# The delta-rule scan: the second half-chunk's tokens kept in the other head's rows, half-chunks issued in turn, and state change and outputs interleaved over the array's quarters

## The reference

```python
def step(S, inp):
    r_t, w_t, k_t, v_t, kk_t, b_t = inp
    sa = jnp.einsum('bhvk,bhk->bhv', S, kk_t)
    S = S * w_t[:, :, None, :] - sa[..., None] * b_t[:, :, None, :] + v_t[..., None] * k_t[:, :, None, :]
    return S, jnp.einsum('bhvk,bhk->bhv', S, r_t)
```

## Time and profile before

| | us |
|---|---|
| median of 3 runs (lowest, highest) | 4899.13 (4895.42, 4918.35) |
| span of the profiled execution | 4902.0 |
| scan of layer 0, from the trace | 354 to about 1080 |
| scan of layer 1, from the trace | 2181 to about 2915 |
| PE busy, whole span | 4470.8 (91%) |
| DVE, ACT, POOL busy, whole span | 3140.0, 2151.1, 1188.4 |

### The profile page before, as it was taken

The page is one execution under the profiler, slowest core; times in us unless marked ns, Lnnn a source line. Parts: engine busy times, 40 slices in busy tenths (PEclk is TensorE's granted clock), DMA queues, the critical chain, the costliest instruction groups (busy, mean ns, idle before and its releaser), DMA issues. The chain is left out here.

```text
span 4902.0 us, 126091 instructions
## 1 busy us (share of the span) xinstructions
PE 4470.8 (91%) x55528; PEld 3812.3 (78%) x55528; DVE 3140.0 (64%) x4910; ACT 2151.1 (44%) x3962; POOL 1188.4 (24%) x863
## 2 busy tenths in 40 slices
PE   6989999989799969989989989799979988999999
PEld 6888888887588858878888878688857657888887
DVE  5436666669788874346666678889864476661752
ACT  2333443432288853334334342688843252331431
POOL 1002222222244420012223221444321000222221
PEclk9999999999899989999999999899989889999999
DMA  5421111123367664321111032567651003333332
GB/s 148 144 63 25 38 23 34 26 85 81 130 257 270 251 204 127 109 59 25 35 34 25 21 108 82 223 247 263 255 180 31 13 1 125 95 101 119 114 113 91
DMA packets 378284, 535.78 MB, mean 109 GB/s; under 512 B 117445, under 2 KB 301829, under 8 KB 349693
## 3 DMA queue, kind: packets, MB, share of 16 engines
q1 hardware_dynamic: 335645, 488.54, 30.8%
q0 software_dynamic: 40752, 33.95, 2.3%
q10 hardware_dynamic: 1344, 5.24, 0.3%
HBM read 569.43 MB, written 121.40 MB: 141 GB/s over the span
## 5 line engine op out<-in xcount | busy, mean ns | idle before, releaser
L289 PE MATMUL ps<-w_hi,xbT 128*128 128x512 f32 x1520 | 498.3, 399 | 19.8 <-DVE w L2835 19.8
L289 PE MATMUL ps<-hT,w_in 128*128 128x416 f32 (+1 forms) x2736 | 495.4, 340 | 4.1 <-DVE hT L3122 4.1
L289 PEld LDWEIGHTS ps<-hT,w_in 128*128 128x128 f32 x2736 | 458.9, 195 | 30.3 <-issue 19.2
L2835 DVE TENSOR_TENSOR w<-w,w_hi 128x2048 fp32r<-128x2048 f32 x190 | 425.6, 2280 | 2.2 <-ACT w_hi L2792 2.2
L1655 POOL TENSOR_TENSOR lm<-Ab,consts 116x416 f32<-116x416 f32 x240 | 255.8, 1073 | 435.9 <-PE ps L289 252.5
L289 PEld LDWEIGHTS ps<-w_hi,xbT 128*128 128x128 f32 x1520 | 288.4, 190 | 87.1 <-DVE w L2835 28.8
L2792 ACT ACTIVATE w_hi<-w 128x2048 fp32r<-128x2048 f32 x190 | 355.4, 1937 | 0.0
L289 PE MATMUL ps<-w,xbT 128*128 128x512 f32 x760 | 299.1, 394 | 0.0
L2866 DVE TENSOR_TENSOR w<-w,w_hi 128x2048 fp32r<-128x2048 f32 x95 | 221.7, 2333 | 95.3 <-ACT w_hi L2828 95.3
L289 PE MATMUL ps<-w_hi,actT 128*128 128x512 f32 x760 | 251.1, 391 | 5.0 <-DVE actT L2861 5.0
L289 PE MATMUL ps<-x1T,w_gate 128*128 128x512 f32 x1056 | 249.5, 393 | 3.2 <-DVE x L4052 1.6
(11 more groups left out here) (463 smaller groups left out, 10868.8 us busy)
## 6 DMA issues: line engine op xcount, KB each, us to landing
w<-in_moe_w_dram SPq DMA_DIRECT2D x192, 1024.0 KB, 12.5
w_gate<-in_w_gate_dram SPq DMA_DIRECT2D x44, 512.0 KB, 3.9
w_up<-in_w_up_dram SPq DMA_DIRECT2D x44, 512.0 KB, 3.9
w_down<-in_w_down_dram SPq DMA_DIRECT2D x44, 512.0 KB, 3.6
w_in<-in_w_in_dram SPq DMA_DIRECT2D x36, 512.0 KB, 4.5
w_out<-in_w_out_dram SPq DMA_DIRECT2D x24, 512.0 KB, 6.8
t_h<-x SPq DMA_DIRECT2D x20, 416.0 KB
kn<-t_kn SPq DMA_DIRECT2D x8, 1040.0 KB, 6.5
```

The costliest lines, as they stand in the source:

```text
L289: made = e.matmul(out, a, b, start=start, stop=stop)
L2835: e.tensor_tensor(w.lo, w.x, w.hf, ALU.subtract).then_inc(*P.c("moe_dve").tick(li, "w13", b, k))
```

## The change

In chunk 1 the tokens of head `o` now lie in the row half of the other head (`token_rows`), so chunk 0 uses the straight pair where chunk 1 uses the crossed one. Phases 11 to 13 issue the chunks in turn (`crossings`), so that four matmuls in a row are on four quarters; ACT takes both turned tensors after both are done. The turn of `hb0` leaves phase 14 and goes behind the level matmuls of phase 22 (`TURN0`), its ACT copy behind that level's `XX`, and phase 23 waits for it. Phases 28 and 31 interleave the state's change (bank `2d`) with the outputs (bank `2d+1`) in `step_rows`. Chunk 1's part of the right side from the values (`value_rows`) and its output from the old state (`state_output`) are made earlier and put away by ACT; DVE then adds the rest (`rh`, `ys`: two more DVE instructions in a step). The waits of `scan_free` become waits for whole groups.

```diff
-BY_ACT = {2, 3, 8, 9} | {13 + 3 * lv for lv in range(4)} | {25 + 4 * x + n for x in range(2) for n in (0, 1, 3)}
+TURN0 = 22
+STATE, INNER = slice(128, 384), slice(384, 512)
...
+def token_rows(o, ch):
+    return half_rows(o ^ ch)
+def crossings():
+    return [(j, ch, o) for j in range(4) for ch in range(2) for o in range(2)]
+def token_turns(P, d, at, x, step, view):
+    return [(P.ps[2 * d + ch][token_rows(o, ch), at + 64 * j:at + 64 * j + 64], view(x, slice(64 * o, 64 * o + 64), j, ch))
+            for j, ch, o in crossings()]
+def state_rows(P, d, m, S, ch):
+    return [(P.ps[2 * d + j % 2][half_rows(o ^ ch ^ j % 2), 64 * (j // 2):64 * (j // 2) + 64],
+             m.kr[64 * o:64 * o + 64, j, 0, H * ch:H * ch + H], S[64 * o:64 * o + 64, j, :], True, ch == 1)
+            for j in range(4) for o in range(2)]
+def value_rows(P, d, m, ch):
+    return [(P.ps[2 * d + j % 2][c, 64 * (j // 2):64 * (j // 2) + 64], m.ak[t, place(1, ch, j), 0, :],
+             m.vt[t, ch, 64 * j:64 * j + 64], ch == 1, True) for j, _, t, c in quarters(range(4))]
+def state_output(P, d, m, S, ch, j):
+    out = P.ps[2 * d + 1][:, STATE]
+    return [(out[half_rows(1 - o), 64 * j:64 * j + 64], m.kr[64 * o:64 * o + 64, j, 1, H * ch:H * ch + H],
+             S[64 * o:64 * o + 64, j, :], True, ch == 1) for o in range(2)]
+def step_rows(P, d, m, S, ch):
+    state, out, mats = P.ps[2 * d][:, STATE], P.ps[2 * d + 1][:, STATE], []
     for j in range(4):
         jc, u = slice(64 * j, 64 * j + 64), place(1, ch, j)
+        if ch == 0:
+            mats += state_output(P, d, m, S, ch, j)
+        for mat, w in ((0, m.ak), (1, m.ab)):
+            for o in range(2):
+                t = token_rows(o, ch)
+                x = m.vt[t, ch, jc] if mat == 0 else m.uu[t, split_columns(j)]
+                mats.append((state[64 * o:64 * o + 64, jc], m.tm[t, mat, ch, jc], x, mat == 0, mat == 1))
+            for o in range(2):
+                t = token_rows(o, ch)
+                x = m.vt[t, ch, jc] if mat == 0 else m.uu[t, split_columns(j)]
+                mats.append((out[half_rows(1 - o), jc], w[t, u, 1, :], x, ch == 1 and mat == 0, mat == 1))
     return mats
...
+        turns(e, P, token_turns(P, d, 0, rw.v, step, lambda x, q, j, ch: x[q, j, half(d, step, ch)]))
+        e.wait_ge(*dv.at(*key, "hb1"))
+        turns(e, P, token_turns(P, d, 256, m.hb, step, lambda x, q, j, ch: x[q, 1, j, H * ch:H * ch + H])
+              ).then_inc(*pe.tick(*key, 3))
+    if ph in (12, 13):
+        mat, use = 13 - ph, 2 * ph - 20
+        if ph == 12:
+            e.wait_ge(*dv.at(*key, "kr1"))
+            e.wait_ge(*ac.at(*key, "ev", 3))
+        else:
+            e.wait_ge(*dv.at(*key, "hb0"))
+            e.wait_ge(*dv.at(*key, "ev", 5))
+        mats = []
+        for j, ch, o in crossings():
+            q, at = slice(64 * o, 64 * o + 64), 2 * H * (place(1, ch, j) // 4 * 2 + j // 2)
+            mats.append((P.ps[2 * d + ch][token_rows(o, ch), at:at + 2 * H].rearrange("p (a t) -> p a t", a=2),
+                         m.hb[q, mat, j, H * ch:H * ch + H], m.kr[q, j, :, H * ch:H * ch + H], True, True))
+        mms(e, mats).then_inc(*pe.tick(*key, use))
...
-            mms(e, mats).then_inc(*pe.tick(*key, base))
+            made = mms(e, mats)
+            if ph == TURN0:
+                made = turns(e, P, token_turns(P, d, 4 * H, m.hb, step, lambda x, q, j, ch: x[q, 0, j, H * ch:H * ch + H]))
...
+            if ph == TURN0 + 1:
+                e.wait_ge(*ac.at(*key, "ev", 8))
             for n in range(4 if lv < 5 else 0):
...
+            if lv == 5 and m.chunks[0] == 1:
+                e.wait_ge(*ac.at(*key, "ev", 2))
+                e.wait_ge(*dv.at(*key, "ev", 7))
+                mats += value_rows(P, d, m, 1)
...
-                e.wait_ge(*ac.at(*key, "ev", use - 1))
+                e.wait_ge(*(ac if ch else dv).at(*key, "y", 0))
+            if ch == 1:
+                e.wait_ge(*ac.at(*key, "values"))
             e.wait_ge(*(dv.at(*key, "fS", x) if step or x else dv.at(li, d, "S0")))
-            mms(e, state_rows(P, d, m, S, ch, m.vt[:, ch, :])).then_inc(*pe.tick(*key, use))
+            mats = state_rows(P, d, m, S, ch)
+            if ch == 0:
+                rest = value_rows(P, d, m, ch)
+                mats = mats[0:4] + rest[0:4] + mats[4:8] + rest[4:8]
+            mms(e, mats).then_inc(*pe.tick(*key, use))
         if part == 1:
-            e.wait_ge(*ac.at(*key, "ev", use))
-            mms(e, [(P.ps[2 * d + j % 2][r, 64 * (j // 2):64 * (j // 2) + 64], m.TT[c, 4 * ch + j, :],
-                     m.rh[c, split_columns(j)], True, True) for j, o, r, c in quarters(range(4))]
-                ).then_inc(*pe.tick(*key, use + 1))
+            e.wait_ge(*(dv if ch else ac).at(*key, "rh", x))
+            mats = [(P.ps[2 * d + j % 2][t, INNER][:, 64 * (j // 2):64 * (j // 2) + 64], m.TT[c, 4 * ch + j, :],
+                     m.rh[c, split_columns(j)], True, True) for j, _, t, c in quarters(range(4))]
+            if ch == 1:
+                for j in range(4):
+                    mats += state_output(P, d, m, S, ch, j)
+            elif x == 0:
+                mats += value_rows(P, d, m, 1)
+            mms(e, mats).then_inc(*pe.tick(*key, use + 1))
         if part == 2:
-            b = scan_bank(P, d, step, use + 2)
-            mats = []
-            for j in range(4):
-                jc = slice(64 * j, 64 * j + 64)
-                mats += [(b[q, jc], m.tm[r, 0, ch, jc], m.vt[r, ch, jc], True, False) for q, r in ODD]
-                mats += [(b[q, jc], m.tm[r, 1, ch, jc], m.uu[r, split_columns(j)], False, True) for q, r in ODD]
-            e.wait_ge(*ac.at(*key, "ev", use + 1))
-            mms(e, mats).then_inc(*pe.tick(*key, use + 2))
-            mms(e, outputs(scan_bank(P, d, step, use + 3), m, S, ch, m.vt[:, ch, :])).then_inc(*pe.tick(*key, use + 3))
+            e.wait_ge(*ac.at(*key, "uu", x))
+            if ch == 1:
+                e.wait_ge(*ac.at(*key, "ys"))
+            elif x == 0:
+                e.wait_ge(*ac.at(*key, "values"))
+            mms(e, step_rows(P, d, m, S, ch)).then_inc(*pe.tick(*key, use + 2))
...
-        take(m.vt[0:HP].rearrange("p c n -> p (c n)"), scan_bank(P, d, step, 2)[0:HP, :], 2)
+        take(m.vt[0:HP], both[:, :, 0:256], 2, 3)
+        take(m.tm[0:HP, 1], both[:, :, 256:512], 3)
...
+    if ph == TURN0:
+        e.wait_ge(*dv.at(*key, "ev", 8 + 3 * level_of(TURN0)[0]))
+        take(m.tm[0:HP, 0], both[:, :, 4 * H:4 * H + 256], 8, 8 + 3 * level_of(TURN0)[0])
+    if ph == 25 and m.chunks[0] == 1:
+        e.wait_ge(*dv.at(*key, "T", 5))
+        e.activation(halves(m.rh)[0:HP], both[:, :, 0:128], ACT.Copy).then_inc(*ac.tick(*key, "values"))
...
+            if x == 0 and ch == 0:
+                e.activation(halves(m.rh)[0:HP], both[:, :, 0:128], ACT.Copy).then_inc(*ac.tick(*key, "values"))
...
+    if ph >= 26:
+        x, part = divmod(ph - 26, 3)
+        ch, use = m.chunks[x], 25 + 4 * x
+        if part == 0 and ch == 1:
+            e.wait_ge(*ac.at(*key, "values"))
+            e.wait_ge(*pe.at(*key, use))
+            e.tensor_tensor(halves(m.rh)[0:HP], halves(m.rh)[0:HP], P.banks[0:HP, 2 * d:2 * d + 2, 0:128], ALU.add).then_inc(
+                *dv.tick(*key, "rh", x))
+        if part == 2:
+            e.wait_ge(*pe.at(*key, use + 2))
+            e.tensor_tensor(m.S[1 - x], m.S[x], P.ps[2 * d][:, STATE].rearrange("p (j n) -> p j n", j=4), ALU.add).then_inc(
+                *dv.tick(*key, "S", x))
+            if ch == 1:
+                e.wait_ge(*ac.at(*key, "ys"))
+                e.tensor_tensor(m.ys[0:HP, 1, :], m.ys[0:HP, 1, :], P.ps[2 * d + 1][0:HP, STATE], ALU.add).then_inc(
+                    *dv.tick(*key, "y", x))
+            if x == 0:
+                e.wait_ge(*ac.at(*key, "f"))
+                e.wait_ge(*dv.at(*key, "S", 0))
+                shrink(1)
```

More of the change, by code:

```diff
@@ L1251, in scan_bank @@
     return P.ps[2 * d + use % 2]
[L1254 to L1259, removed]
 def squares(ps):
@@ L1318, in quarters @@
     return [(j, o, half_rows(o), half_rows(o ^ j % 2)) for j in js for o in range(2)]
[L1321 to L1331, removed]
@@ L1358, in scan_pe @@
         out = [scan_bank(P, d, step, use)[:, 0:416].rearrange("p (j t) -> p j t", t=C) for use in range(2)]
-        for use in range(2):
-            scan_free(e, P, li, d, step, use)
+        if step:
+            e.wait_ge(*dv.at(li, d, step - 1, "S", 1))
+            e.wait_ge(*(dv if m.chunks[1] else ac).at(li, d, step - 1, "y", 1))
         for j in range(4):
@@ L1367, in scan_pe @@
         e.wait_ge(*dv.at(*key, "kr0"))
[L1368 to L1387, removed]
-                     m.hb[q, mat, j, hs], m.kr[q, j, :, hs], True, True) for j in range(4) for q, r in ODD]
-                ).then_inc(*pe.tick(*key, use))
+        turns(e, P, token_turns(P, d, 0, rw.v, step, lambda x, q, j, ch: x[q, j, half(d, step, ch)]))
@@ L1405, in scan_pe @@
             if lv == 1:
```

(37 more changed lines are left out.)

48 lines of the change are left out of this document (15 added, 33 removed).

## The result

The changed kernel takes 4919.14 us (median of 20 runs, 4907.56 to 4942.78) against 4901.97 of the kernel before (20 runs, 4890.33 to 4921.78); the ratio is 1.0035, 95% interval 1.0025 to 1.0046. So it is 0.35% slower, clear of noise though inside the half per cent that the prediction calls no change, and 122 us above the forecast. The profiled execution of the changed kernel is the slowest of its twenty (4942.78 us, a span of 4941.0); the one of before lies near its median. Its granted clock over the whole program is 0.932, where the median of the twenty is 0.936 and the kernel before has 0.958. So the loss of clock that follows is in every execution, but the trace shows it some 20 us larger than the median execution has it ((0.936 - 0.932) x 4941).

What follows compares the result with a forecast made beforehand. PE was taken to bound the scan except where DVE sets the time up to the second `Ab`. Savings of 4.71 us a step, net 2.54, gave 102 us in 40 steps: span 4902.0 to 4800, time 4797 us, range 4735 to 4862.

Steps and rivals of the forecast that it cites:

- net sum of 2.54 us a step: Whole scan step: PE time saved less what waits take back, 2.54 us, or 102 us in 40 steps.
- the clock falls: Rival: long PE waits before the second `Ab` halve the clock; 4831 to 4874 us in part (0.10), slower each step (0.03).
- saving of 4.71: PE time saved per step by four quarters in phases 11 to 14, 28 and 31: 4.71 us, 188 in 40 steps.
- (1): Turns and first products ahead of the second `Ab`: DVE sets the time there, so 0 of 1.67 us counted.
- (2): Phase 13 waits for both `Ab`, not the first: 0.3 us a step lost (0 to 0.5).
- (3): Turn of `hb0` in phase 22, its copy delaying phase 23: covered by the `sig` to `kr0` chain, 0.45 us given back.
- (4): First chunk's end: state change complete only with the last matmul, DVE instructions follow; 0.3 us lost (0 to 1.3).
- (5): Before phase 28, PE waits for ACT's second copy behind `uu`: 0.35 us lost (0 to 0.4).
- (6): Two added DVE instructions, 0.42 us each, lie where DVE waits for PE: 0 lost (to 0.5).
- signs of being wrong: First durations not halving, `sig` to `kr0` changing by a microsecond, or the scans' granted clock below 0.95.
- The quarters do not run side by side: Rival: four-quarter groups gain nothing of the saving and new waits remain, 38 us, giving 4937 us; chance 0.05.
- PE bounds everywhere: Rival: the wait for `Ab` moves with PE, so 3.5 to 4.7 us a step, 4710 to 4759 us; chance 0.08.

Runs made afterwards that it cites:

- ends_only: Kernel before, with only phases 28 and 31 alternating outputs and state change over the quarters; phases 11 to 14 and copies unchanged: 4911.87 us, ratio 1.0019.
- chunk_ends_apart: Kernel of `front_by_chunk` with phases 28 and 31 issued one product after the other: 4898.82 us, ratio 0.9986.
- front_by_chunk: Changed kernel with phases 11 to 13 issued chunk by chunk on one pair of quarters, each chunk with its own signal and wait: 4884.61 us, ratio 0.9963.
- feed: Kernel before plus 2048 constant matmuls ahead of the first scan (512 pair, 1024 four quarters, 512 pair): 3.45 to 3.73 us per 64 on four quarters.

## Why the prediction was wrong

**The step that failed** is the net sum of 2.54 us a step: it has no term for the clock. The fall stood beside it as the rival *the clock falls*, at 0.10 in part and 0.03 in full. I argued from two single waits, 1.49 without a fall and 2.49 with one, for "one wait of 2 us or more" at 20 of 40 places, 34 us. What the runs show in its place: the clock took 103.6 us more. In the front the rival's price was near (14 falls, 37.5 us), from two pauses in a row, 1.30 and 1.85, rather than one of 2. The rest came where I had looked for none: behind the copy of `hb0` in layer 1 (23.9), behind "issue" (22 more) and in the first steps (14 more). In the mean of the 40 steps it is 5.2 us at half clock, and the prediction gave 5.1 as the point from which the kernel becomes slower. So the mechanism and its price stood there; its chance and its places were wrong. The Trainium skill, TensorE: Matmul & The Clock Gate, A second HAM failure mode, tells of short idle times between groups of matmuls that make the clock swing; the fall inside the pause of 1.85, behind one of 1.30, agrees in direction.

**What was not in it at all** is the supply of instructions. The durations of four quarters came from 8 records, too few to run dry; "issue" grew by 35.7 us (53.3 - 17.6), 0.9 a step. `ends_only` and `chunk_ends_apart` show where: with the ends interleaved "issue" is 45 to 56 us in every run, with the ends apart 18 to 28.

**By term.** The saving of 4.71 was near (4.6 by the books, 4.2 without half clock in pauses); the ends' 1.7 gave 1.6 of work, and in time between 14 us gained and 8 lost. (1) held in kind: in layer 0 PE's waits ahead of phases 12 and 13 grew by some 25 us, 1.2 of the 1.67 a step. But only 6.6 of it is for `Ab` (10.4 to 17.0, not to 30); the rest is for ACT's copies. (2) was 0.3 and measured 0.5 alone, since phase 12's wait for the copies counts beside it. (3) failed: in layer 1 PE waits ahead of phase 23 for the copy of the turn, most of 23.6 us or 1.1 a step, where 0.45 was to be given back. In layer 0 PE does not wait there, but DVE waits longer for the exponential behind that copy, 1.34 in place of 1.11 us in every second step. (4), the waits for `S`, are 2.6 us in layer 0's 20 steps, 0.13 against 0.3 (of the 5.2 in the row above, two of 1.3 stand ahead of phase 12), and 5.5, or 0.27, in layer 1. (5), the second copy behind `uu` (`rh` at one chunk, `ys` at the other), is 4.7 + 4.2 us in layer 0, 0.45 against 0.35. (6) held: none of PE's waits is for DVE's `rh` or `ys`. All new waits without "issue" come to 66 us (102.0 - 35.7), 1.7 a step; the prediction had 2.2. Two of its signs of being wrong came: the clock of the scans fell to 0.91, and in layer 0 `sig` to `kr0` grew by 0.8 us in the mean and by over a microsecond in six steps. *The quarters do not run side by side* was wrong (0.49 us for 16 turns), *PE bounds everywhere* too: taking work away made the kernel slower, and giving some back faster.

What stays open: how much time each kind of pause costs through the clock. The traces say what stood ahead of each fall, and the runs take away the falls of the front (`front_by_chunk`) or show those of "issue" without them (`ends_only`); no run takes away the waits for the copy of `hb0` without bringing others.

## What to carry to other kernels

Work saved on an engine that has to wait behind it is idle time, and on TensorE that may be paid twice, once as the wait and once at half clock; cost every new pause with the work that follows it, not by its own length. When matmuls get shorter, count how many follow one another and compare with what the instruction queue brings before believing a rate read from a few of them. Speed up the stretches with work queued, and where another engine sets the time leave the groups long, with a signal for each part.

## What the runs showed of the hardware

I had not expected that TensorE's instructions come in blocks of 256, 64 of these float32 matmuls, one block in 3.45 to 3.73 us when it waits for them (`feed`), so that below some 56 ns a matmul a longer run gains nothing from the array. In the changed kernel's scan each of the 68 pauses in "issue" ends 1.19 to 1.61 us behind such a block's packet. In `feed` the granted clock was 1.00 from 394 to 437 us, with a pause of 1.45 to 1.72 behind every block; behind the pause of 2.00 at 441.36 it was 0.50 for 3.4 us:

```profile
394.00:437.40 43.40, 24.08 (x1540) 22.38 (x1540) 0.00 (x0) 0.00 (x0) 0.00 (x0) 1.00 0.02 5
441.90:445.30 3.40, 2.66 (x106) 2.47 (x96) 0.00 (x0) 0.00 (x0) 0.00 (x0) 0.50 0.02 5
```
